# Two places for arriving weights and four for prepared ones, with each unit rounded one unit sooner

## The reference, cut to what matters

```python
# block 1, layers 0 and 1
x = x + (mixer_attn_rglru(...) if l % 2 == 0 else pool_mixer(...))
x = x + memory_xattn(rms_norm(x, g), mem_n, w_q, w_kv, q_g, k_g, w_o)
x = x + sq_relu_mlp(rms_norm(x, g), w1, w2)          # 1024 -> 4096 -> 1024
# block 2, layers 0 and 1
h = x + 0.5 * swiglu(rms_norm_2(x, g), w1, w3, w2)   # 1024 -> 2816 -> 1024
p = rms_norm_2(h, g) @ w_in    # conv module, window attention, memory attention
h = h + y @ w_out
h = h + 0.5 * swiglu(rms_norm_2(h, g), w1, w3, w2)
x = rms_norm_2(h, final_g)
```

## Time and profile before

| what | us |
|---|---|
| median of 3 runs | 1743.68 |
| lowest and highest run | 1743.01, 1745.07 |
| the profiled execution | 1742.12 |
| its span, first to last instruction | 1740.8 |
| TensorE busy | 1683.9 |
| VectorE busy | 1232.8 |
| ScalarE busy | 892.8 |

### The profile page before, as it was taken

One profiled execution on the slowest core, in us unless ns is written; L12 is line 12 of the kernel. 1 busy time (PEld: TensorE's weight loads), 2 busy tenths in 40 slices (PEclk: granted clock), 3 DMA queues, 4 the chain that ended last, 5 costly groups with the idle time before them and its releaser, 6 DMA issues.

```text
span 1740.8 us, 24401 instructions
## 1 busy us (share of the span) xinstructions
PE 1683.9 (97%) x10136; PEld 1487.6 (85%) x10136; DVE 1232.8 (71%) x1487; ACT 892.8 (51%) x1149; POOL 183.2 (11%) x166
## 2 busy tenths in 40 slices
PE   7999999999999999999999899999999999899997
PEld 6889988888998888888889688888888898788886
DVE  7985577765657767677767767778777667677764
ACT  6554455444545554455444555556555545455542
POOL 0401010011101001100021010003100111010002
PEclk9999999999999999999999899999999999999999
DMA  7444345545434555555554215555555542145551
GB/s 280 162 160 143 120 165 194 191 179 211 159 112 166 194 210 182 186 183 190 194 179 149 73 57 210 194 200 189 179 196 187 194 172 107 49 149 189 184 197 55
DMA packets 41439, 291.09 MB, mean 167 GB/s; under 512 B 4720, under 2 KB 4976, under 8 KB 7024
## 3 DMA queue, kind: packets, MB, share of 16 engines
q1 hardware_dynamic: 39456, 282.61, 45.0%
q10 hardware_dynamic: 1872, 6.92, 1.0%
HBM read 288.46 MB, written 1.05 MB: 166 GB/s over the span
## 4 chain that ended last, share of the span: by engine, by line
PE 81%; DVE 11%; ACT 4%; POOL 2%; issue 2%; DMA 0%; ACTq 0%; DVEq 0%; POOLq 0%
PE ps L298 36%; PE ps L297 18%; DVE w_lo L1399 4%; PE ps L295 4%; PE ps L286 3%; PE ps L288 3%; PE ps L287 3%; PE ps L331 2%; PE ps L333 2%; PE ps L332 2%; PE ps L296 2%; DVE xT L1407 2%; ACT w_hi L888 1%; POOL stat L2054 1%; PE ps L437 1%
## 5 line engine op out<-in xcount | busy, mean ns | idle before, releaser
L1399 DVE TENSOR_TENSOR w_lo<-raw,w_hi 128x2048 fp32r<-128x2048 f32 x268 | 613.5, 2292 | 229.8 <-ACT w_hi L888 226.1
L298 PE MATMUL ps<-xT,w_hi 128*128 128x512 f32 x1736 | 620.6, 397 | 0.0
L888 ACT ACTIVATE w_hi<-raw 128x2048 fp32r<-128x2048 f32 x268 | 510.0, 1904 | 215.6 <-PE ps L298 117.7
L297 PE MATMUL ps<-xT,w_lo 128*128 128x256 f32 x1736 | 485.5, 280 | 0.0
L298 PE MATMUL ps<-hT,w_hi 128*128 128x512 f32 x1168 | 412.6, 397 | 0.0
L298 PEld LDWEIGHTS ps<-xT,w_hi 128*128 128x128 f32 x1736 | 326.9, 188 | 67.6
L297 PEld LDWEIGHTS ps<-xT,w_lo 128*128 128x128 f32 x1736 | 328.4, 189 | 11.5
L297 PE MATMUL ps<-hT,w_lo 128*128 128x256 f32 x1168 | 327.2, 280 | 1.7 <-DVE hT L1584 1.7
L298 PEld LDWEIGHTS ps<-hT,w_hi 128*128 128x128 f32 x1168 | 219.3, 188 | 51.0
L297 PEld LDWEIGHTS ps<-hT,w_lo 128*128 128x128 f32 x1168 | 220.3, 189 | 5.0 <-DVE hT L1584 2.9
L940 ACT ACTIVATE tmp<-ps 128x512 f32<-128x512 f32 x120 | 72.0, 600 | 257.5 <-PE ps L298 257.5
(11 more groups left out here) (254 smaller groups left out, 2057.4 us busy)
## 6 DMA issues: line engine op xcount, KB each, us to landing
raw<-weights_dram SPq DMA_DIRECT2D x264, 1024.0 KB, 4.8
raw<-weights_dram SPq DMA_DIRECT2D x4, 768.0 KB, 4.1
tmp<-mem_dram ACTq DMA_DIRECT2D x2, 1024.0 KB, 6.6
x<-x_in_dram SPq DMA_DIRECT2D x2, 512.0 KB, 5.8
raw<-weights_dram SPq DMA_DIRECT2D x2, 512.0 KB, 6.7
arena<-mem_dram ACTq DMA_DIRECT2D x1, 1024.0 KB, 7.9
arena<-pool_mat_dram ACTq DMA_DIRECT2D x1, 1024.0 KB, 4.8
tmp<-masks_dram ACTq DMA_DIRECT2D x1, 768.0 KB, 8.4
```

Of the source, the lines that this page charges most:

```text
L297: pe.matmul(ps[:, bank, 0:S], lo, src[:, k, 0, :], start=False, stop=False)
L298: return pe.matmul(ps[:, bank, :].rearrange("p (a n) -> p a n", a=2), hi, src[:, k, :, :], start=False, stop=last)
L888: act.activation(b.w_hi[:, s, 0:w], b.raw[:, s, 0:w], ACT.Copy).then_inc(*mark("hi", u))
L1399: dve.tensor_tensor(b.w_lo[:, s, 0:w], b.raw[:, s, 0:w], b.w_hi[:, s, 0:w].bitcast(F32), ALU.subtract).then_inc(*mark("lo", u))
```

## The change

The weights as they come have two places, the high and low parts have four. Unit `u` now lies in place `u % 2` of `raw` and `u % 4` of the others. The load of unit `u` waits for the low part of unit `u - 2`, the high part for the end of TensorE's unit `u - 4`. From the call with 12 on, `highs(n)` and `lows(n)` prepare the units up to `n + 1`; the calls themselves stay where they are.

```diff
-SLOTS = 3
+SLOTS, RAW_SLOTS = 4, 2
+
+AHEAD_FROM = 12
...
-        self.raw = sb("raw", [P, SLOTS, UNIT])
+        self.raw = sb("raw", [P, RAW_SLOTS, UNIT])
...
+def prepared(upto):
+    return min(upto + (upto >= AHEAD_FROM), N_UNITS - 1)
...
     def highs(upto):
-        while done_units[0] <= min(upto, N_UNITS - 1):
+        while done_units[0] <= prepared(upto):
             u = done_units[0]
             s, w = u % SLOTS, width(u)
-            act.wait_ge(*at("d_w%d" % s, u))
+            act.wait_ge(*at("d_w%d" % (u % RAW_SLOTS), u))
             if u >= SLOTS:
                 act.wait_ge(*at("unit", u - SLOTS))
-            act.activation(b.w_hi[:, s, 0:w], b.raw[:, s, 0:w], ACT.Copy).then_inc(*mark("hi", u))
+            act.activation(b.w_hi[:, s, 0:w], b.raw[:, u % RAW_SLOTS, 0:w], ACT.Copy).then_inc(*mark("hi", u))
...
     def lows(upto):
-        while done_units[0] <= min(upto, N_UNITS - 1):
+        while done_units[0] <= prepared(upto):
...
-            dve.tensor_tensor(b.w_lo[:, s, 0:w], b.raw[:, s, 0:w], b.w_hi[:, s, 0:w].bitcast(F32),
+            dve.tensor_tensor(b.w_lo[:, s, 0:w], b.raw[:, u % RAW_SLOTS, 0:w], b.w_hi[:, s, 0:w].bitcast(F32),
...
     for u in range(1, N_UNITS):
-        s, w = u % SLOTS, width(u)
-        if u >= SLOTS:
-            sp.wait_ge(*(at("lo", u - SLOTS) if u > SLOTS else at("lo_half", 1)))
+        s, w = u % RAW_SLOTS, width(u)
+        if u >= RAW_SLOTS:
+            sp.wait_ge(*(at("lo", u - RAW_SLOTS) if u > RAW_SLOTS else at("lo_half", 1)))
         sp.dma_start(b.raw[:, s, 0:w], d["weights"][u, :, 0:w]).then_inc(*landed("d_w%d" % s, u))
```

## The result

| | us |
|---|---|
| before, 6 runs | 1745.07 (1743.01 to 1749.47) |
| after, 6 runs | 1760.29 (1757.06 to 1764.54) |
| ratio after / before | 1.008, 95% interval 1.0066 to 1.0094 |
| profiled execution after | 1760.66, span 1759.1 (before 1742.12, 1740.8) |

The change costs 0.8%. I had said 1760.

The account below looks back on a forecast made before the run. TensorE, busy 1683.9 of 1740.8 us, was taken as the bound, with loads tied to low parts. 1.2 + 7.0 - 3.4 + 3.3 + 3.3 + 5.1 = 16.5 on 1743.7 gave 1760; range 1755 to 1765 (60 in 100), wider 1750 to 1769.

Parts of the forecast that it names:

- The shift: From unit 13 on, each load keeps its time but its high part is wanted one step sooner; hidden in feed-forward, 0.
- The start: First units: load of unit 4 waits for low part of 2, delaying diagonal and spread 1.2 us; bounds 0.6 and 4.8.
- The switch: Call with 12: extra units and a tied load delay the row maxima, 7.0 us; lower end 2.3 (extra low part), upper 10.6.
- The ends of the output projections: After output projections TensorE finds the next unit prepared: 3.4 us won, 0.7 of it before layer 0's cross attention.
- The gated diagonal: Second gated feed-forward, both layers: `lows(v + 3)` waits for its load ahead of the diagonal, delaying spread 3.3 us each.
- The clock: Half-clock stretches behind three new TensorE stops, 1.7 us each, 5.1 in all; ends 0 and 3.4 each.
- that two places are enough: Rival: no load ends last anywhere, so only the five stops go, 6.5 us won, 1737.2; 6 in 100.
- That the switch is hidden: Rival: the pair at 12 to 14 costs only its extra low part, 1753.8 us; 12 in 100.
- That the stops stay: Rival: the five stops come from VectorE's low parts of `x`, so 3.4 is not won, 1763.6 us; 4 in 100.
- That it comes out about even: Rival: diagonals and switch half hidden and no clock loss, near 1746 us; 6 in 100.
- That the clock stays low for two stretches: Rival: two half-clock stretches after each stop instead of one, 1765.3 us; 12 in 100.

Follow-up runs that it names:

- e10: Changed kernel with the advance from the call with 20 and the diagonal ahead of `lows(v + 3)`, the same kernel run a second time: 1744.27 us.
- e5: Changed kernel with the advance from the call with 20 and the diagonal ahead of `lows(v + 3)`, first run: 1744.49 us, ratio 1.0002 to before.
- e12: Changed kernel, advance from 20, diagonal ahead of `lows(v + 3)`, loads of units 2, 3 and 4 waiting as with three places: 1743.30 us, ratio 1.0005.
- e2: Changed kernel with the advance beginning at the call with 20 instead of 12: 1751.23 us.
- e6: Changed kernel, advance still from 12, but low parts overwrite the arriving weights in five shared places, so loads wait only for TensorE: 1740.50 us.
- e3: Changed kernel with the diagonal ahead of `lows(v + 3)` in the first step of every gated feed-forward: 1751.59 us.
- e7: Changed kernel with raw weights and low parts in five shared places and no unit prepared sooner than before the change: 1740.72 us.
- e11: Changed kernel with five shared places for raw and low parts, advance from 20, diagonal ahead of `lows(v + 3)`, run a second time: 1734.04 us.
- e1: Changed kernel with its two raw and four other places, but no unit prepared sooner than before: 1750.71 us, ratio 1.0038 to before.
- e9: Changed kernel, advance from 20, diagonal ahead of `lows(v + 3)`, unit 2 alone arriving in the fourth low-part place: 1744.81 us.

## Why the prediction was right, point by point

**The shift, 0.** The chain of reasoning held: the five stops gone, high parts waiting for loads 27 times, nothing lost in steady feed-forward.

**1. The start, +1.2: too small.** The step that failed is "The load of unit 4 now waits for the low part of unit 2, which ends at 24.1". The wait is true, but the load of unit 2 itself, which waited for nothing with three places, now waits for the halves of unit 0. High part 2 came 5.3 later, and low part 2 ended at 25.8. And the load of unit 2 took 7.5 us, where I had 4.8 for a load. "DMA: Bandwidth & Descriptors" of the Trainium skill (Issuing engines are not separate DMA queues) says that transfers issued by different engines run on the same 16 DMA engines. The traces agree: a weight load took 4.8 us in the median, and in the first 40 us, where the tables and the memory are loaded too, 7.5 in before, 6.1 in after and 7.1 in e10. The start measured 2.8, and 1.5 more of half clock. The 2.8 is one draw: the same start put spread 1.0 us (e5) to 4.3 us (e10) later than in the earlier trace rows, which my bounds of 0.6 and 4.8 hold. e12 shows that the loads of units 2 to 4 are the cause.

**2. The switch, +7.0: measured 7.1.** e2 won 9.1 with the clock, and e6 parts it: about 2.2 is the extra low part, as in my lower end, the rest the load of 14 behind the low part of 12. The maxima came at 103.6 and not near 100.4, but only because the start was 4.3 late and not 1.2.

**3. The ends of the output projections, -3.4: measured -1.1, -1.25, -1.1,** so -3.45. The split was a little off: the cross attention gave 1.1 where I had allowed 0.7.

**4. The gated diagonal, +3.3 twice: measured 2.6 and 2.5.** The delay behind the pair of low parts was exact: 11.8 us from their start to the diagonal (1046.80 to 1058.63) against 8.6 in the earlier trace rows. What I mis-sized is where I started to count: the pair began 0.7 us earlier, relative to TensorE, than before. So "TensorE arrives at about 1046.8 and idles about 5" became 4.2, in two pieces: 1.6 at L388 and 2.6 at L404. The first piece I had put at nothing: GpSimd's last addition falls beside a low part now. In the changed kernel TensorE would else have waited for it at spread, so it costs nothing more there; with the diagonal first (e3, e5) it takes back what the two stops would have given.

**5. The clock, +5.1: measured 6.7 net.** 1.5 at the start, which I had not listed, 1.85, 1.55 and 1.85 behind the three stops that I had, 1.65 in the window attention, and 1.7 back. The size of one, 1.7, was right; e3 removes two of the stops and their stretches together. That one would come behind each of the three stops was not to be had from the earlier trace rows: that stop of 2.17 us stands in all fourteen traces, and a half-clock stretch follows within 2 us of it in only four of them (before, e2, e7, e11). In the kernel after, the eight transposes behind it took 1.09 at full clock. What decides it stays open, and that three came where I had three is in part luck.

By parts: 2.8 + 7.1 - 3.45 + 5.1 + 6.7 = 18.25 of 18.3 us of span. Against these two traces the small start and the small clock (1.6 short each) outweigh the large item 4 (1.5 over). Against the medians of six runs each, the difference was 15.2 and not 16.5, and the kernel before had 1745.1 and not the 1743.7 on which I had put it; the two errors cancel. The mechanism and the size of the switch were right. That the time itself came out within 0.3 us is luck.

The rivals: that two places are enough fell with e1 (still 5.6 slower without the advance). That the switch is hidden fell with e2. That the stops stay fell with the trace. That it comes out about even fell with the result; its own terms (1.2 + 3.5 - 3.4 + 3.3) make 1748.3 and not 1746, outside the 3.5 us that I called none. That the clock stays low for two stretches came true once, behind the longest stop, but 2.9 of its 6.8 us lay in the stop itself.

## What to carry to other kernels

Count a buffer's places by what ends last for each: with two places a load hangs on the conversion of the unit before the last, and every burst of conversions then contains a load, wherever it stands. Preparing sooner gained 3.7 us here with free loads and nothing with tied ones, and each unit that is prepared sooner stands ahead of something: so first move the urgent short step ahead of the long one. Leave a prepared place unused where an engine would else stand behind TensorE for it (2.9 us here). Where a conversion can be written over its source, the place serves both, and the load need not wait for it: that turned 1760 into 1740, and 1734 with the advance from 20 and the diagonal first.

## What I had not expected of the hardware

**A small GpSimd step takes 2.6 us beside VectorE's low part.** The root on 128 x 2 elements, before and after, at the start:

```profile
29.37 2.60 POOL L2054 TENSOR_TENSOR stat<-stat,mhalf 128x2 f32<-128x2 f32 x1 [28.54 <-DVE stat L1433]
```
```profile
31.06 0.70 POOL L2060 TENSOR_TENSOR stat<-stat,mhalf 128x2 f32<-128x2 f32 x1 [30.23 <-DVE stat L1439]
```

Before, VectorE's low part ran beside it (29.13 to 31.41) and it took 2.60; after, VectorE was waiting for a load and it took 0.70. The same holds in the other traces: 0.70 in all six with the start of the kernel after, 2.60 in the rest, e9 and e12 among them, with the low part beside it. So part of the late load was paid back: VectorE's idle time made the root 1.9 us shorter. At L388 the same effect cost: an addition on 128 x 256 elements took 2.59 beside a low part instead of 0.74. "GPSIMD Engine Reference" of the Trainium skill (1. Specifications) says that the two engines share their access to SBUF and contend when VectorE reads two inputs from it. The trace agrees, and the low part reads two.

**Loads at the start vary.** The diagonal of one kernel came at 33.0 in one execution and at 36.3 in another (e5, e10), which alone is more than most effects that I tried to resolve there; one trace of each kernel does not settle an effect of 1 us at that place.
